# A fused transformer block on one core: the down stage of its FFNs with a fourth split slot, another order of products, and the sum T3 made by an adding DMA

## Chip, cores and metric

The kernel runs on one core of a Trainium2 chip. The metric is the device time of one execution in microseconds. Lower is better.

## What is computed

One block of depth 1 over a sequence of 256 tokens with 2048 channels, all in float32: an FFN, a mixer (sparse attention beside a gated delta rule), and a second FFN, each added to the scaled residual and normalised. The change touches only the two FFNs, and of them only the last product:

```python
D_MODEL = 2048; SEQ = 256; D_FF = 5632

def swiglu(x, w_gate, w_up, w_down):
    return (jax.nn.silu(x @ w_gate) * (x @ w_up)) @ w_down

h = layer_norm(DEEPNORM_ALPHA * h + 0.5 * swiglu(h, ffn1_w_gate[l], ffn1_w_up[l], ffn1_w_down[l]), ...)
```

## The kernel before, in words

**Matmuls of split operands.** Each float32 operand is split into a high and a low part, and a product is three matmuls: high by high, high by low, low by high. The weights come as *raw* tiles of two k-tiles by 512 columns (128 x 1024 elements, 512 KB). SyncE loads them into eight raw slots (L857 in the down stage), ScalarE writes the high part (`split_hi`, L444; `form_hi`, L1054), VectorE the low part as raw minus high (`split_lo`, L451; `form_lo`, L1173), into three split slots (`whi`, `wlo`). TensorE uses them and counts `unit_used`; ScalarE waits on that count before it writes a slot again. SyncE waits for the low half (`lo_done`) of the item that read a raw slot last before it loads that slot again. The queues are in order.

**The down stage.** h (256 tokens x 5632) by w_down (5632 x 2048) is done in two pairs of column chunks: phases F1DA and F1DB in the first FFN, F2DA and F2DB in the second. The class `Pair` (from L50) writes the order of the work out. Its `items` are the work of ScalarE, VectorE and TensorE in order, its `raws` the loads of SyncE in order. An item is either a *unit* (u, c), one raw tile used for both token tiles: 12 matmuls; or one of the products P1 to P7 of a *quad*, 6 matmuls. A quad takes two row tiles a = 4 + q and b = 8 + q and both column chunks of the pair, a 2 by 2 block of weights against a 2 by 2 block of h (two row groups by two token tiles), and makes the eight block products with seven, by Winograd's form of Strassen's scheme. The first pair has three quads, the second four, so there are 14 quads in the kernel.

**The sums of a quad.** VectorE makes four sums of raw weight tiles in `add` (L1146): P5 from (a, 1) and (a, 0) (L1156), P7 from (b, 1) and (a, 1), written over the raw tile (a, 1) (L1159), P6 from (b, 1) and P5's sum (L1162), P4 from (b, 0) and P6's sum (L1167). P5, P6 and P4's sums have a third each of the tile `sumB`. The sums of h (S1 to S4, from A11, A12, A21, A22) are made once in each FFN, beside the first items of the first pair: `sums` (L1195) on VectorE, with `sum_hi` on ScalarE (L1061) and `sum_lo` on VectorE (L1192).

**Order before.** The first pair has 10 units at its head; then a quad lies as unit, P1, P5, unit, P7, P3, unit, P6, P2, unit, P4, and after the last quad come plain units (the tail). P7 and P6's sums are made just before the low half of the item they follow or that is next.

**Folds.** P1, P5, P6 and P7 gather in four PSUM banks `tp`, the others in the units' banks `acc0`, `acc1`. In the tail of each pair ScalarE copies P1's bank (L1083) and VectorE folds the banks into the residual (`fold`, L1252: L1249, L1258, L1261, L1268).

**Edges.** The last six items of the second pair are plain units whose halves go to six slots of their own (`edge`), so that the next phase can start on the split slots.

**Pool.** Pool (GpSimd) has nothing in the down stages but the loads of the norm's gain and bias (`norm_gains`, L778), which wait for a unit of the second pair, and then the norm's reciprocal roots (L783). Its part is written out at L2651 to L2663.

```python
self.raws += [(a, 0), (a, 1), some[0], (b, 1), some[1], (b, 0), *some[2:]]
forms = [("P1", "P5"), ("P7", "P3"), ("P6", "P2"), ("P4",)]
```

## Time and profile before

| | us |
|---|---|
| median of 3 runs | 1941.09 (1940.5 to 1942.88) |
| the profiled execution: its own time | 1941.81 |
| its span, from the first to the last instruction | 1939.8 |
| TensorE busy | 1909.5 (98%) |
| VectorE busy | 1253.9 (65%) |
| ScalarE busy | 894.1 (46%) |
| Pool busy | 66.9 (3%) |
| HBM traffic over the span | 184 GB/s |

The profile's page and the trace's answers give times in us from the span's start. PE is TensorE, PEld its weight loads, DVE VectorE, ACT ScalarE, POOL GpSimd, SP SyncE; L451 is line 451 of the kernel. The first FFN's down stage lies at 495 to 732 us, the second's at 1688 to 1929 us. In an instruction's row, the first number is its start, the second its duration, and the square brackets tell how long the engine was idle before it and what released it.

### The profile page before, as it was taken

The numbers are of one execution on the slowest core, as the hardware profiler recorded it, in microseconds if no ns is written. First come the engines' busy times: TensorE is split into PE (matmuls) and PEld (weight loads), VectorE is DVE, ScalarE is ACT, GpSimd is POOL, SyncE is SP. The second block draws the span as 40 slices with busy tenths as digits, with TensorE's granted clock in tenths as the row PEclk, the third lists the DMA queues.
The fourth block names the chain that finished last, engine by engine and source line by source line (L and its number), as shares of the span: only waits on it lengthen the run. The fifth ranks groups of instructions, "written<-read, shape, count | busy, mean of one in ns | idle before, by whom it ended". The sixth has DMA issues, their size and how long they took to land.

```text
span 1939.8 us, 27987 instructions
## 1 busy us (share of the span) xinstructions
PE 1909.5 (98%) x10490; PEld 1617.4 (83%) x10490; DVE 1253.9 (65%) x1411; ACT 894.1 (46%) x996; POOL 66.9 (3%) x93
## 2 busy tenths in 40 slices
PE   9999999999999999999999999999999999999997
PEld 8888888888778778999999888888888888877776
DVE  5555554555887887676766958555554555587887
ACT  5444443444454553545644544444444444455452
POOL 0000000000000001300131000000000000000000
PEclk9999999999999999999999999999999999999999
DMA  8666666667565665655442067566666666545654
GB/s 304 193 187 189 189 185 189 178 193 235 157 211 182 214 219 171 212 181 161 127 133 89 23 225 243 171 186 182 186 190 197 192 187 188 189 163 184 206 190 168
DMA packets 185365, 357.37 MB, mean 184 GB/s; under 512 B 11328, under 2 KB 23616, under 8 KB 184272
## 3 DMA queue, kind: packets, MB, share of 16 engines
q1 hardware_dynamic: 183600, 347.43, 57.4%
q0 software_dynamic: 1696, 8.99, 1.4%
q8 instruction: 47, 0.77, 0.2%
q14 instruction: 22, 0.18, 0.0%
HBM read 354.28 MB, written 2.10 MB: 184 GB/s over the span
## 4 chain that ended last, share of the span: by engine, by line
PE 91%; DVE 5%; issue 1%; DMA 1%; ACT 1%; POOL 0%; POOLq 0%; SPq 0%; DVEq 0%; ACTq 0%
PE acc L463 23%; PE acc L465 23%; PE acc L464 23%; PE acc L486 3%; PE acc L488 3%; PE acc L490 3%; PE tp L985 1%; PE tp L987 1%; PE tp L986 1%; DVE wlo L451 1%; PE tp L917 1%; PE acc L985 1%; PE acc L987 1%; PE acc L986 1%; ACT whi L444 1%
## 5 line engine op out<-in xcount | busy, mean ns | idle before, releaser
L451 DVE TENSOR_TENSOR wlo<-raw,whi 128x1024 fp32r<-128x1024 f32 (+2 forms) x579 | 692.5, 1202 | 602.8 <-ACT whi L444 600.7
L444 ACT ACTIVATE whi<-raw 128x1024 fp32r<-128x1024 f32 (+2 forms) x579 | 596.6, 1037 | 815.3 <-PE acc L465 726.9
L463 PE MATMUL acc<-whi,xT 128*128 128x512 f32 (+2 forms) x1644 | 631.0, 384 | 0.8 <-ACT zab L1612 0.4
L465 PE MATMUL acc<-whi,xT 128*128 128x512 f32 (+2 forms) x1644 | 625.7, 381 | 0.0
L464 PE MATMUL acc<-wlo,xT 128*128 128x512 f32 (+2 forms) x1644 | 625.2, 380 | 0.0
L463 PEld LDWEIGHTS acc<-whi,xT 128*128 128x128 f32 x1644 | 308.7, 188 | 64.7 <-issue 1.8
L465 PEld LDWEIGHTS acc<-whi,xT 128*128 128x128 f32 x1644 | 308.7, 188 | 59.5
L464 PEld LDWEIGHTS acc<-wlo,xT 128*128 128x128 f32 x1644 | 308.9, 188 | 55.8
L463 PE MATMUL acc<-whi,hT 128*128 128x512 f32 x432 | 170.8, 395 | 6.7 <-DVE wlo L451 6.7
L464 PE MATMUL acc<-wlo,hT 128*128 128x512 f32 x432 | 168.4, 390 | 0.0
L465 PE MATMUL acc<-whi,hT 128*128 128x512 f32 x432 | 168.4, 390 | 0.0
L486 PE MATMUL acc<-xT,whi 128*128 128x256 f32 x384 | 108.7, 283 | 0.0
L488 PE MATMUL acc<-xT,whi 128*128 128x256 f32 x384 | 108.7, 283 | 0.0
L490 PE MATMUL acc<-xT,wlo 128*128 128x256 f32 x384 | 108.7, 283 | 0.0
L463 PEld LDWEIGHTS acc<-whi,hT 128*128 128x128 f32 x432 | 81.1, 188 | 32.8 <-DVE wlo L451 16.4
L465 PEld LDWEIGHTS acc<-whi,hT 128*128 128x128 f32 x432 | 81.1, 188 | 17.4
L464 PEld LDWEIGHTS acc<-wlo,hT 128*128 128x128 f32 x432 | 81.2, 188 | 15.4
L1054 ACT ACTIVATE whi<-raw 128x1024 fp32r<-128x1024 f32 x56 | 59.4, 1061 | 39.3 <-PE acc L465 25.1
L1173 DVE TENSOR_TENSOR wlo<-raw,whi 128x1024 fp32r<-128x1024 f32 x56 | 67.4, 1221 | 11.6 <-ACT whi L1054 10.2
L490 PEld LDWEIGHTS acc<-xT,wlo 128*128 128x128 f32 x384 | 73.7, 192 | 0.0
L488 PEld LDWEIGHTS acc<-xT,whi 128*128 128x128 f32 x384 | 73.7, 192 | 0.0
L486 PEld LDWEIGHTS acc<-xT,whi 128*128 128x128 f32 x384 | 73.7, 192 | 0.0
(345 smaller groups left out, 1854.6 us busy)
## 6 DMA issues: line engine op xcount, KB each, us to landing
raw<-in_ffn_w_down_dram SPq DMA_DIRECT2D x176, 512.0 KB, 4.7
raw<-in_ffn_w_up_dram SPq DMA_DIRECT2D x175, 512.0 KB, 3.7
raw<-in_ffn_w_gate_dram SPq DMA_DIRECT2D x174, 512.0 KB, 3.8
raw<-in_w_in_dram SPq DMA_DIRECT2D x48, 512.0 KB, 3.9
raw<-in_w_out_dram SPq DMA_DIRECT2D x32, 512.0 KB, 6.4
raw<-in_w_in_dram SPq DMA_DIRECT2D x32, 260.0 KB, 2.8
raw<-in_w_in_dram SPq DMA_DIRECT2D x16, 456.0 KB, 5.2
raw<-in_w_q_idx_dram SPq DMA_DIRECT2D x8, 512.0 KB, 3.8
```

The costliest lines, as they stand in the source:

```text
L444: act.activation(hi[:, s, :, 0:w], raw[:, r, :, 0:w], ACT.Copy).then_inc(hi_done, 1)
L451: dve.tensor_tensor(lo[:, s, :, 0:w], raw[:, r, :, 0:w], hi[:, s, :, 0:w].bitcast(F32), ALU.subtract).then_inc(lo_done, 1)
L463: pe.matmul(o, hi, w_hi[:, s, k, 0:width], start=first and k == 0, stop=False)
L464: pe.matmul(o, hi, w_lo[:, s, k, 0:width], start=False, stop=False)
L465: ins = pe.matmul(o, lo, w_hi[:, s, k, 0:width], start=False, stop=last and k == UNIT_KT - 1)
L486: pe.matmul(o, whi[:, s, k, cols], hi, start=first and k == 0 and c == 0, stop=False, skip_group_check=True)
L488: pe.matmul(o, whi[:, s, k, cols], lo, start=False, stop=False, skip_group_check=True)
L490: ins = pe.matmul(o, wlo[:, s, k, cols], hi, start=False, stop=end, skip_group_check=True)
L985: pe.matmul(o, x_hi, w_hi[:, s, k], start=i == touches[0] and k == 0, stop=False)
L986: pe.matmul(o, x_hi, w_lo[:, s, k], start=False, stop=False)
L1054: act.activation(w_hi[:, s], form_raw(p, i), ACT.Copy).then_inc(hi_done, 1)
L1173: dve.tensor_tensor(w_lo[:, s], form_raw(p, i), w_hi[:, s].bitcast(F32), ALU.subtract)\
```

## The change

In each quad the products come in another order: unit, P1, P3, P5, unit, P7, P6, unit, P2, P4, unit. The order of the loads follows. The first pair's head has 13 units instead of 10, and the second pair's last quad four units around it instead of three.

From item 16 of the first pair on (the first quad's P5) there is a fourth split slot, in the room of two of the three parts of `sumB`; it serves both pairs. The remaining part, `form_sum`, holds P5's sum and later P4's. P6's sum is written over the raw tile (a, 0), the *corner*. VectorE waits for both halves of the item that read these places before. The raw tiles (a, 0) and (b, 0) are therefore free only with the item ahead of P4, and (b, 1) with the one ahead of P6.

The signs of the sums are turned so that every weight sum of a quad adds. T3, P7's operand, was (b, 1) - (a, 1) by VectorE and is now (a, 1) + (b, 1): Pool issues a DMA that reads (b, 1) from HBM and adds it onto the raw tile (a, 1), once P5's sum has read it. ScalarE waits for its landing before P7's high half. VectorE's instruction is gone. The signs of two sums of h and of the folds into the second chunk change with it.

The sums of h are spread over items 2 to 14 instead of 2 to 9. VectorE makes a weight sum two items ahead of its product. The folds are eight instructions of 512 columns in place of six and one of 1024.

```diff
-            self.raws += [(a, 0), (a, 1), some[0], (b, 1), some[1], (b, 0), *some[2:]]
-            forms = [("P1", "P5"), ("P7", "P3"), ("P6", "P2"), ("P4",)]
+            self.raws += [some[0], (a, 0), (b, 1), (a, 1), *some[1:3], (b, 0), *some[3:]]
+            forms = [("P1", "P3", "P5"), ("P7", "P6"), ("P2", "P4"), ()]
...
     def released_by(self, r):
-        return max(i for i, (what, _, _) in enumerate(self.items)
-                   if what not in ("P4", "P5", "P6") and self.raw_of(i) == r)
+        last = max(i for i, (what, _, _) in enumerate(self.items)
+                   if what not in ("P4", "P5") and self.raw_of(i) == r)
+        for q, (a, b) in enumerate(self.quads):
+            if self.raws[r] in ((a, 0), (b, 0)):
+                return max(last, self.item("P4", q) - 1)
+            if self.raws[r] == (b, 1):
+                return max(last, self.item("P6", q) - 1)
+        return last
...
+def split_slots(pairs, one_more_from, kept_apart):
+    free, places = list(range(SPLIT_SLOTS)), [{}, {}]
+    user = {}
+    for pair, plan in enumerate(pairs):
+        for i in range(len(plan.items) - (kept_apart if pair else 0)):
+            if (pair, i) == (0, one_more_from):
+                free.insert(0, SPLIT_SLOTS)
+            s = free.pop(0)
+            free.append(s)
+            places[pair][i] = s, user.get(s)
+            user[s] = pair, i
+    return places, user
...
-    PAIRS = [Pair(QUADS[:3], sorted(ENDS + [7, 11]), sorted(ENDS + [7, 11]), 10, (4, 4, 4)),
-             Pair(QUADS, ENDS, ENDS, 2, (4, 4, 4, 3))]
+    PAIRS = [Pair(QUADS[:3], sorted(ENDS + [7, 11]), sorted(ENDS + [7, 11]), 13, (4, 4, 4)),
+             Pair(QUADS, ENDS, ENDS, 2, (4, 4, 4, 4))]
+    FOURTH_FROM = 16
...
+        form_sum = mz("form_sum", 88, [P, UNIT_KT, BANK])
+        fourth_hi = mz("fourth_hi", 92, [P, 1, UNIT_KT, BANK], F32R)
+        fourth_lo = mz("fourth_lo", 96, [P, 1, UNIT_KT, BANK], F32R)
...
+        def down_pool(pool, f, w_down):
+            down_v = w_down.rearrange("(k p) n -> p k n", p=P)
+            for pair, p in enumerate(DOWN[f]):
+                plan = PAIRS[pair]
+                for q, (a, b) in enumerate(plan.quads):
+                    right = raw_ready(pool, p, a, 1)
+                    pool.wait_ge(sem("formed"), made(f, p, "P5", q))
+                    if right_added(f, p, q) > 16:
+                        pool.wait_ge(sem("right_added"), right_added(f, p, q) - 16)
+                    col = (2 * pair + 1) * BANK
+                    pool.dma_start(right, down_v[:, 2 * b:2 * b + 2, col:col + BANK], accum_op=ALU.add)\
+                        .then_inc(sem("right_added"), 16)
...
-                if name in MADE:
+                if name == "P7":
+                    act.wait_ge(sem("right_added"), right_added(f, p, q))
+                elif name in MADE:
                     act.wait_ge(sem("formed"), made(f, p, name, q))
...
                 if name == "P5":
-                    dve.tensor_tensor(sumB[:, 0], upper, left, ALU.subtract).then_inc(sem("formed"), 1)
-                if name == "P7":
-                    block, right = raw_ready(dve, p, b, 1), raw_ready(dve, p, a, 1)
-                    dve.tensor_tensor(right, block, right, ALU.subtract).then_inc(sem("formed"), 1)
+                    dve.tensor_tensor(form_sum[:], upper, corner, ALU.add).then_inc(sem("formed"), 1)
                 if name == "P6":
+                    block = raw_ready(dve, p, b, 1)
+                    dve.wait_ge(lo_done, st.index(p, 0, plan.item("P1", q) + 1))
+                    dve.wait_ge(hi_done, st.index(p, 0, plan.item("P1", q) + 1))
                     dve.wait_ge(sem("formed"), made(f, p, "P5", q))
+                    dve.tensor_tensor(corner, block, form_sum[:], ALU.add).then_inc(sem("formed"), 1)
                 if name == "P4":
                     left = raw_ready(dve, p, b, 0)
+                    dve.wait_ge(lo_done, st.index(p, 0, plan.item("P5", q) + 1))
                     dve.wait_ge(sem("formed"), made(f, p, "P6", q))
-                    dve.tensor_tensor(sumB[:, 2], left, sumB[:, 1], ALU.subtract).then_inc(sem("formed"), 1)
+                    dve.tensor_tensor(form_sum[:], left, corner, ALU.add).then_inc(sem("formed"), 1)
...
-                    if what == "P7":
-                        add(p, "P6", q)
-                    if after[0] == "P6":
-                        add(p, "P4", after[1])
...
+                    soon, of, _ = plan.items[min(i + 2, len(plan.items) - 1)]
+                    if soon in MADE:
+                        add(p, soon, of)
...
+            down_pool(pool, 0, ffn1_w_down[0])
             pool.wait_ge(unit_used, gains_free(0))
             norm_gains(pool, ln1_g, ln1_b)
             norm_pool(pool, 0)
             mixer_pool(pool)
+            down_pool(pool, 1, ffn2_w_down[0])
```

## Rows read from the trace of the kernel before

**Rows 1.** The page, parts 1 and 2: busy time; granted clock in 40 slices.
```profile
PE 1909.5 (98%) x10490; PEld 1617.4 (83%) x10490; DVE 1253.9 (65%) x1411; ACT 894.1 (46%) x996; POOL 66.9 (3%) x93
...
PEclk9999999999999999999999999999999999999999
```

**Rows 2.** Stretches: us, busy of PE, PEld, DVE, ACT, POOL, clock, DMA share, GB/s.
```profile
495.00:610.00 115.00, 112.18 (x494) 91.02 (x493) 97.53 (x89) 59.11 (x57) 0.00 (x0) 1.00 0.53 171
610.00:725.00 115.00, 112.18 (x487) 90.11 (x486) 94.63 (x89) 60.32 (x58) 1.28 (x2) 1.00 0.64 218
554.00:562.00 8.00, 6.89 (x30) 5.37 (x30) 5.21 (x5) 3.90 (x4) 0.00 (x0) 1.00 0.89 269
```

**Rows 3.** TensorE's waits, whole span: us in total, times, longest.
```profile
PE acc L463 <- DVE wlo L451: 6.7, 6, 1.7
PE acc L985 <- DVE wlo L1173: 2.4, 2, 1.2
...
PE acc L463 <- DVE edge L451: 1.6, 2, 0.8
...
PE tp L985 <- DVE wlo L1173: 1.4, 2, 1.1
```

**Rows 4.** Timeline of TensorE: the first matmul behind three of the waits.
```profile
524.90 0.50 PE L463 MATMUL acc<-whi,hT 128*128 128x512 f32 x1 [1.71 <-DVE wlo L451]
...
558.04 0.50 PE L463 MATMUL acc<-whi,hT 128*128 128x512 f32 x1 [1.11 <-DVE wlo L451]
...
673.82 0.47 PE L985 MATMUL acc<-whi,sumA 128*128 128x512 f32 x1 [1.20 <-DVE wlo L1173]
```

**Rows 5.** Timeline of VectorE ahead of the wait at 524.90 us.
```profile
508.28 1.22 DVE L927 TENSOR_TENSOR hT<-tp,hT 128x1024 fp32r<-128x1024 f32 x1
509.42 1.22 DVE L1182 TENSOR_TENSOR sumB<-hT 128x1024 f32<-128x1024 f32 x1
...
523.62 1.22 DVE L451 TENSOR_TENSOR wlo<-raw,whi 128x1024 fp32r<-128x1024 f32 x1
```

**Rows 6.** Timeline of ScalarE and VectorE: halves of units, then of products.
```profile
489.66 1.06 ACT L444 ACTIVATE whi<-raw 128x1024 fp32r<-128x1024 f32 x1 [1.66 <-PE acc L465]
...
490.76 1.23 DVE L451 TENSOR_TENSOR wlo<-raw,whi 128x1024 fp32r<-128x1024 f32 x1 [1.49 <-ACT whi L444]
...
492.38 1.06 ACT L444 ACTIVATE whi<-raw 128x1024 fp32r<-128x1024 f32 x1 [1.66 <-PE acc L465]
...
550.12 1.06 ACT L1054 ACTIVATE whi<-raw 128x1024 fp32r<-128x1024 f32 x1 [0.30 <-PE tp L987]
551.48 1.06 ACT L1054 ACTIVATE whi<-raw 128x1024 fp32r<-128x1024 f32 x1 [0.30 <-PE tp L987]
555.66 1.06 ACT L444 ACTIVATE whi<-raw 128x1024 fp32r<-128x1024 f32 x1 [3.13 <-PE tp L987]
```

**Rows 7.** Groups by line: count, then busy us, mean ns, idle before.
```profile
L1159 DVE TENSOR_TENSOR raw<-raw 128x1024 f32<-128x1024 f32 x14 | 17.0, 1216 | 0.0
...
L1249 DVE SCALAR_TENSOR_TENSOR resid<-sumB,resid 128x512 f32<-128x512 f32 x16 | 10.6, 686 | 0.1
```

**Rows 8.** DMA issues of Pool's queue: count, KB each, median us to landing.
```profile
ln_g<-in_ln_g_dram POOLq DMA_DIRECT2D x3, 1024.0 KB, 8.0
...
wuk<-in_w_uk_dram POOLq DMA_DIRECT2D x1, 1024.0 KB, 5.5
...
cq_g<-in_q_norm_g_dram POOLq DMA_DIRECT2D x1, 256.0 KB, 3.9
```

**Rows 9.** Timeline of Pool: its first load in a down stage.
```profile
706.91 0.74 POOL L778 DMA_DIRECT2D ln_g<-in_ln_g_dram  x1 [705.47 <-PE acc L465]
```

**Rows 10.** The down loads' line, L857, of all down stages.
```profile
DMA to landing us min/median/max: 3.4/4.7/10.3
```

**Rows 11.** Timeline of SyncE's queue, 553 to 555 us.
```profile
553.37 2.02 SPq L857 DMA_DIRECT2D raw<-in_ffn_w_down_dram  x4
```

**Rows 12.** The chain of waits from 608 to 620 us: start, us, what.
```profile
610.56 6.52 DMA raw<-in_ffn_w_down_dram
```

More of the change, by code:

```diff
@@ L71, in __init__ @@
                 self.items += [(form, q, 0) for form in forms[k]]
-        self.tail = len(self.items)
+        self.tail = 1 + max(i for i, item in enumerate(self.items) if item[0] == "P4")
         plain(len(units))
@@ L403, in split_place @@
                 return edge_hi, edge_lo, slot, st.index(p, 0, edge_free(slot))
+            if plan_of(p) is not None:
+                f, pair = (0, 1)[p in DOWN[1]], (0, 1)[p in (F1DB, F2DB)]
+                s, before = SPLITS[pair][u] if u < n else (u - n, LAST_USER[u - n])
+                if before is not None:
+                    free = st.index(DOWN[f][before[0]], 0, before[1] + 1)
+                elif s < SPLIT_SLOTS:
+                    last = [v for v in range(2 * KU) if ring_place(v, 2 * KU, SPLIT_SLOTS) == s][-1]
+                    free = st.index(GU[f], GATE_CHUNKS - 1, last + 1)
+                else:
+                    free = None
+                return (whi, wlo, s, free) if s < SPLIT_SLOTS else (fourth_hi, fourth_lo, 0, free)
             if p in EXITS and isinstance(it, int) and it == st.phases[p].iters - 1:
@@ L882, in made, with right_added @@
             pair = DOWN[f].index(p)
-            return F_STEPS * f + len(SUM_STEPS) + sum(PAIR_STEPS[:pair]) + 4 * q + MADE[name]
+            return F_STEPS * f + len(SUM_STEPS) + sum(PAIR_STEPS[:pair]) + ADDS * q + MADE[name]
         def folded(f, pair, n):
-            return F_STEPS * f + len(SUM_STEPS) + sum(PAIR_STEPS[:pair]) + 4 * len(PAIRS[pair].quads) + n
+            return F_STEPS * f + len(SUM_STEPS) + sum(PAIR_STEPS[:pair]) + ADDS * len(PAIRS[pair].quads) + n
+        def right_added(f, p, q):
+            pair = DOWN[f].index(p)
+            quads = [len(plan.quads) for plan in PAIRS]
+            return 16 * (sum(quads) * f + sum(quads[:pair]) + q + 1)
+        def down_pool(pool, f, w_down):
[10 more added lines that the diff above has]
+                        .then_inc(sem("right_added"), 16)
         def p_free(f, pair):
@@ L1052, in form_hi @@
                     act.wait_ge(raw_loaded[v % RAW_SLOTS], st.loaded(p, 0, v))
-                act.wait_ge(unit_used, free)
+                if free is None:
+                    act.wait_ge(sem("formed"), summed(f, "S4 low"))
+                else:
+                    act.wait_ge(unit_used, free)
                 act.activation(w_hi[:, s], form_raw(p, i), ACT.Copy).then_inc(hi_done, 1)
@@ L1146, in add @@
             def add(p, name, q):
-                first = p == DOWN[f][0] and q == 0
-                a, b = plan_of(p).quads[q]
+                pair, plan = DOWN[f].index(p), plan_of(p)
+                a, b = plan.quads[q]
+                corner = raw_ready(dve, p, a, 0)
                 if name == "P5":
-                    upper, left = raw_ready(dve, p, a, 1), raw_ready(dve, p, a, 0)
-                    if first:
-                        dve.wait_ge(sem("formed"), summed(f, "S4 low"))
-                    elif q == 0:
-                        dve.wait_ge(sem("formed"), folded(f, 0, FOLDS))
-                    dve.tensor_tensor(sumB[:, 0], upper, left, ALU.subtract).then_inc(sem("formed"), 1)
@@ L1157, in add @@
-                if name == "P7":
-                    block, right = raw_ready(dve, p, b, 1), raw_ready(dve, p, a, 1)
-                    dve.tensor_tensor(right, block, right, ALU.subtract).then_inc(sem("formed"), 1)
+                    upper = raw_ready(dve, p, a, 1)
+                    if q > 0:
+                        dve.wait_ge(lo_done, st.index(p, 0, plan.item("P4", q - 1) + 1))
+                        dve.wait_ge(hi_done, st.index(p, 0, plan.item("P4", q - 1) + 1))
+                    else:
+                        dve.wait_ge(sem("formed"), folded(f, 0, FOLDS) if pair else summed(f, "S4 low"))
@@ L1288, in down_pair @@
                 for i in range(LEAD if pair == 0 else 0, len(plan.items)):
-                    what, q, _ = plan.items[i]
-                    after = plan.items[i + 1] if i + 1 < len(plan.items) else ("", 0, 0)
-                    if after[0] == "P1":
-                        add(p, "P5", after[1])
-                    if what == "P5":
-                        add(p, "P7", q)
-                    if what == "P7":
-                        add(p, "P6", q)
-                    if after[0] == "P6":
-                        add(p, "P4", after[1])
-                    if what == "unit":
+                    if plan.items[i][0] == "unit":
                         split_lo(dve, p, 0, i)
```

79 lines of the change are left out of this document (44 added, 35 removed).

## Prediction

> **What bounds the kernel now.** I read the page first, then the stages, then the waits inside the down stages. TensorE is busy 98% of the span and the granted clock is full, 2.4 GHz [rows 1]. So only TensorE's idle time can be won, and only work that makes TensorE late can cost. The two halves of the first down stage show 112.2 us of matmuls in 115 us each, with VectorE at 95 to 98 us of 115 [rows 2]. TensorE's waits name the rest: over both down stages 6.7 + 2.4 + 1.6 + 1.4 = 12.1 us, all released by VectorE's low half of a split [rows 3]. They fall on a unit behind the sums, on items behind P4 and on an edge unit; the larger ones of the first stage are the rows at 524.90, 558.04 and 673.82 us, and the second stage repeats them [rows 4]. These 12.1 us are the whole prize (the first matmul behind a wait also takes 0.50 instead of 0.39 us [rows 4], so up to 2 us more).
>
> The mechanism of one item: ScalarE's high half starts when a slot comes free, takes 1.06 us, VectorE's low half starts 1.10 us after it and takes 1.23 us, and back to back VectorE needs 1.14 us per instruction [rows 5, 6]. A unit (12 matmuls) holds TensorE 2.72 us and a product (6) 1.36 us, the spacing of ScalarE's starts in the two cases [rows 6]. The work on TensorE is the same before and after: the same units and the same seven products a quad.
>
> **The change, part by part.**
>
> *The sums of the second operand and the head of 13 units.* Before the longest stall, VectorE works without a break from 508.28 on, and the low half of the unit at 523.62 comes 1.7 us late [rows 5, 4]. The sums are the same number of instructions, but now lie over items 2 to 14, with the P5 sum behind item 14. A unit with two instructions costs VectorE 2.28 us against 2.72 us of TensorE, and the few items with three catch up before item 14. I take this stall (1.7 us, once per down stage) as gone; the bound is that it stays.
>
> *One VectorE instruction fewer a quad.* The T3 subtraction (L1159) is 1.22 us, 14 times [rows 7], 16 us of VectorE at the back-to-back pace. What it covers is only the stalls above; VectorE has idle time otherwise. The folds become eight instructions of 0.68 us instead of six and one of full size, 1.22 us [rows 7]: 0.14 us more, four times, beside TensorE's work; nothing, and 0.1 us at the kernel's end if that cover were gone.
>
> *The fourth slot.* Before the stall at 558 us ScalarE waited 3.1 us for TensorE to free a slot [rows 6], and VectorE then for ScalarE; the one at 674 us is of this kind [rows 4]. A slot more lets the high half go one item earlier, 1.36 us or more. I take these as gone too. It exists only from item 16 on, when the last low half of S4 is written. The new waits of the P5, P6 and P4 sums are for halves that stand earlier in VectorE's own queue, as the sums share one buffer and the corner's block: they hold nothing up, and their price is the raw slots kept longer, below.
>
> *The adding DMA.* Nothing like it is in the trace, so it is bounded. It is issued by Pool behind the P5 sum, because that sum reads the block which the DMA overwrites; ScalarE's half of P7 waits for its landing, and behind that wait ScalarE holds P6, a unit, P2 and P4, and VectorE all their low halves. Pool's queue has nothing else in the down stages; the gains' loads come at 706.91 us [rows 9], behind the last adding DMA, so they don't collide. Landings of Pool's DMAs: 3.9 us for 256 KB, 5.5 us for 1 MB, 8.0 us for 1 MB beside the down stage's own loads [rows 8]. The adding DMA writes 512 KB but must read 1 MB, the weights and the block. Lower end: it costs as a plain 512 KB, between 3.9 and 5.5, so 4.4 us; upper end: 8.0 us, as the 1 MB beside loads. I take 7.0 us, nearer to the rows with contention, since the 16 DMA engines are 53 to 64% busy there [rows 2]; with 0.2 us for the two semaphores D = 7.2 us from P5's sum to the landing. Issuing costs Pool 0.7 us of it [rows 9] and no other engine.
>
> The Trainium skill (DMA: Bandwidth & Descriptors, Anatomy of one DMA) gives 2.0 us plus bytes at 436 GB/s for a DMA of this queue, 4.4 us for the 1 MB; the trace has 5.5 to 8.0 us for 1 MB, and the trace decides. The skill (Collectives: The Full Stack, The bandwidth ceiling) says that an adding transfer is half as fast since it needs two source reads, not because of the addition; no row here shows it.
>
> *What covers it.* The first quad still has three slots, and its P5 sum stands behind P1's low half and S4's. ScalarE starts P1's high half 0.2 us after TensorE begins the unit two before P1, 5.4 us ahead of P1. Then 1.3 us to the low half (with a little queueing), 1.14 to S4's, 1.25 to the P5 sum, 1.23 for it: it ends 5.1 us after that point, 0.3 us before P1 starts. P1, P3, P5 and a unit last 3 x 1.36 + 2.72 = 6.8 us, and P7's two halves need 2.4 us ahead of P7. Cover: 0.3 + 6.8 - 2.4 = 4.7 us. D = 7.2 exceeds it by 2.5 us.
>
> In later quads there is a loop. The new order releases six loads at once, when P2's low half of the quad before is done: the blocks at its corner and left are kept for the sums until then, and the queue is in order. The third load of the six is the block (a, 1), which the P5 sum needs. A load alone lands in 3.4 us at least [rows 10]; in a burst of four issued from 553.37 us on [rows 11] the 8 us that follow move 269 GB/s [rows 2], which is 1.95 us per 512 KB; at 400 GB/s it would be 1.3; I take 1.6. The third lands 0.2 + 3.4 + 3.2 = 6.8 us after the release. Then: P5 sum 1.25; adding DMA D; P7's halves 2.4; VectorE's four instructions up to P2's low half (P6, unit, the P4 sum, P2) 4 x 1.13 = 4.5. The loop is 6.8 + 1.25 + 2.4 + 4.5 + D = 15.0 + D. TensorE's quad is 4 x 2.72 + 7 x 1.36 = 20.4 us. So D may be 5.4 us; with 7.2 the stall is 1.8 us a quad.
>
> **Sum.** Loops: 2 in the first pair, 3 in the second, 5 x 1.8 = 9 us; the first quad 2.5 us; the second pair's first quad has units ahead of it and the P5 sum early, 0. That makes 11.5 us a down stage, 23 us for both. Taken away: 12.1 us. Net +10.9 us. The profiled execution took 1941.8 us (span 1939.8 and 2.0 around it), 0.7 us over the median of 1941.1; so 1952.7 by the profile, 1952 as a median.
>
> **The rivals.**
>
> *Covered (the other side).* If D is at most 4.7 us and the burst lands as fast as single loads, no stall of either kind is left: 1941.1 - 12.1 - 2 = 1927. For it: 3.9 us for 256 KB, 5.5 us for 1 MB [rows 8], and nothing in the trace forbids the adding unit to run at the rate of a load. With D from 4.7 to 5.4 only the first quad stalls, at most 0.7 us twice. Against it: six loads are in the queue just then, and a Pool DMA beside loads took 8.0 us [rows 8]. The point from which it decides: D plus the third load's landing under about 12 us. The skill's 4.4 us of the DMA page, taken as it is, would give this case; the rows so far bear it out badly. Chance 0.34.
>
> *Balance.* D about 6.2 us: 5 x 0.8 + 1.5 = 5.5 us a down stage, 11 for both against 12.1: 1940. The same result comes if the change doesn't do what it says, the old stalls staying because ScalarE gets no slot in time, and the DMA just covered. Chance 0.15.
>
> *The loads become the bound.* The burst of six behaves as the loads at 610 us did: issued one behind the other, the one that ScalarE waited for took 6.5 us [rows 12], and the worst down load of the kernel 10.3 us [rows 10]. If the third of six lands at 8.5 instead of 6.8 and slows the adding DMA to 7.8: loop 24.5, stall 4.1 a quad, 5 x 4.1 + 3.1 = 24 us a stage, 47 against 12: 1976. ScalarE's waits would then name the plain loads too. Chance 0.13.
>
> *Forecast* (D 6.5 to 8.2): 1943 to 1964 by the same sum, 12 us of kernel time per us of D (10 from the loops, 2 from the first quads). Chance 0.38.
>
> **Numbers.** The likeliest case gives 1952 us. The range takes in the covered case (1927, and 1925 with the slowed matmuls) and goes up to 1968, past D = 8.2; most of the loads' case lies above. A measurement of this kernel tells 0.2%, 3.9 us, from no change. Faster: 0.34 and a little of the balance, 0.35. Same: 0.14. Slower: 0.38 + 0.13, 0.51. Cases of both signs hold most of the chance; the forecast's own range is 1943 to 1964.
>
> **What would show it.** The rows of Pool should have 14 issues into the raw tile with a time to landing: 7 us for my forecast, under 5 for the covered case. ScalarE's waits should have a new group on these DMAs, of 1 to 3 us each, and TensorE idle ahead of the P7 products (the line of the products, into the transposes' tile) 12 times. The waits on VectorE's low halves at the old places (the unit behind the sums, the unit behind P4, the edge) should be gone; if one stays, its part above is wrong. SyncE should issue six loads within 2.5 us once a quad, and the landings of the down loads should rise above their median of 4.7 us [rows 10]. If TensorE shows no idle time ahead of P7 while the DMA takes 7 us, my loop is wrong, not D. If the stall is there and the DMA lands in 5 us, it is the loads.

## The result, and the profile after

The changed kernel takes **1964.8 us** (median of 4 runs, 1964.45 to 1966.21). The kernel before, on the same chip, takes 1941.9 us (4 runs, 1940.5 to 1942.88). The ratio is 1.012, with a 95% interval from 1.0102 to 1.0138: slower by 23 us. The forecast was 1952 us, in a range from 1925 to 1968 us. The sign was right. The size was not: +23 us against a forecast of +10.9 us. The profiled execution took 1966.2 us, with a span of 1964.5 us. Two versions below had one slow execution each among their ten (5191 us in experiment 4, 2342 us in experiment 11); comparisons leave these out.

The page of the changed kernel, the lines that answer to [rows 1, 7, 8] (parts 1, 2, 5 and 6):

```profile
PE 1918.1 (98%) x10490; PEld 1629.1 (83%) x10490; DVE 1239.9 (63%) x1401; ACT 889.6 (45%) x996; POOL 83.8 (4%) x107
...
L1121 ACT ACTIVATE whi<-raw 128x1024 fp32r<-128x1024 f32 x54 | 56.2, 1054 | 78.8 <-DMA raw<-in_ffn_w_down_dram 67.9
...
L949 POOL DMA_DIRECT2D raw<-in_ffn_w_down_dram x14 | 17.0, 1216 | 1371.3 <-DVE form_sum L1226 844.0
...
raw<-in_ffn_w_down_dram SPq DMA_DIRECT2D x176, 512.0 KB, 6.8
...
raw<-in_ffn_w_down_dram POOLq DMA_DIRECT2D x14, 512.0 KB, 7.6
```

VectorE has 14 us less work and TensorE the same 10,490 matmuls, yet these are 8.6 us *longer* in sum than in [rows 1]. ScalarE stands for 67.9 us before high halves that come from raw tiles. The plain down loads land in 6.8 us in the median, against 4.7 us in [rows 10]. The 14 adding DMAs land in 7.6 us, and an issue costs Pool 1.2 us instead of the 0.74 us of [rows 9].

TensorE's waits, whole span, the lines that answer to [rows 3]: us in total, times, longest.

```profile
PE tp L1047 <- DVE wlo L1243: 26.3, 10, 4.5
...
PE tp L1047 <- DVE fourth_lo L1243: 2.9, 2, 1.7
...
PE tp L616 <- DVE resid L781: 0.8, 1, 0.8
```

L1047 into `tp`, released by a product's low half (L1243), is P7. None of the places of [rows 3] is left; in their stead P7 is late 12 times, by 26.3 + 2.9 = 29.2 us in all. The timeline of one such place, the second quad of the first stage, for ScalarE, VectorE and Pool:

```profile
552.07 1.06 ACT L1121 ACTIVATE whi<-raw 128x1024 fp32r<-128x1024 f32 x1 [2.11 <-DMA raw<-in_ffn_w_down_dram]
...
554.80 1.23 DVE L1226 TENSOR_TENSOR form_sum<-raw 128x1024 f32<-128x1024 f32 x1 [0.42 <-DMA raw<-in_ffn_w_down_dram]
...
556.59 1.22 POOL L949 DMA_DIRECT2D raw<-in_ffn_w_down_dram  x1 [20.57 <-DVE form_sum L1226]
...
564.13 2.00 ACT L1121 ACTIVATE whi<-raw 128x1024 fp32r<-128x1024 f32 x2 [6.02 <-DMA raw<-in_ffn_w_down_dram]
```

P1's block has landed at 552.07 us. The P5 sum runs from 554.80 to 556.03 us. The square brackets say that the sum was released by a load's landing, the block (a, 1), and not by VectorE's own queue. Pool issues the adding DMA 0.56 us later, and ScalarE can start P7's high half at 564.13 us, 8.1 us behind the sum. TensorE in the same place:

```profile
566.59 0.77 PE L1047 MATMUL tp<-whi,sumA 128*128 128x512 f32 x1 [2.84 <-DVE wlo L1243]
567.16 0.63 PE L1048 MATMUL tp<-wlo,sumA 128*128 128x512 f32 x1
567.58 0.63 PE L1049 MATMUL tp<-whi,sumA 128*128 128x512 f32 x1
```

This is what the forecast had no term for. Behind a wait of 2.84 us the matmuls take 0.63 us each and start 0.43 us apart, where they otherwise take 0.39 us and start 0.23 us apart. The windows of TensorE show why: us, busy, granted clock, DMA share, GB/s.

```profile
495.00:610.00 115.00, 108.90 (x476) 0.99 0.59 183
610.00:725.00 115.00, 108.11 (x461) 0.97 0.66 216
...
566.60:570.10 3.50, 3.50 (x9) 0.53 0.02 5
570.20:590.00 19.80, 18.63 (x82) 1.00 0.75 238
705.40:710.00 4.60, 4.60 (x13) 0.63 0.00 0
```

The granted clock falls to its lower level, 1.2 GHz, for a few us, and is back at 2.4 GHz after that. This happens behind six of the twelve waits: those of 2.84, 1.86 and 3.64 us in the first stage and of 4.45, 4.28 and 3.54 us in the second. In the profile of before it happens in no down stage; the first two windows had a clock of 1.00 in [rows 2]. A spell (a stretch of matmuls at the lower level) holds about eight slow matmuls in the first stage and ten to thirteen in the second, 0.20 us more each. That is 1.6 us a spell and 2.0 to 2.6 us, some 12 us altogether.

Not all of these 12 us are a cost, as the starts of the first three P7 show:

```profile
543.10 0.47 PE L1047 MATMUL tp<-whi,sumA 128*128 128x512 f32 x1 [2.02 <-DVE wlo L1243]
...
566.59 0.77 PE L1047 MATMUL tp<-whi,sumA 128*128 128x512 f32 x1 [2.84 <-DVE wlo L1243]
...
590.08 0.47 PE L1047 MATMUL tp<-fourth_hi,sumA 128*128 128x512 f32 x1 [1.25 <-DVE fourth_lo L1243]
```

From the first to the second lie 23.49 us without a spell, from the second to the third 23.49 us with one. The spell made the next wait shorter (1.25 us instead of 2.84), not the quad longer. What sets P7's start runs through the loads, the P5 sum, the adding DMA and the halves, and not through TensorE: in all ten later quads the first load of the quad's burst is issued 6.9 us after the high half of the P7 before started, with a spell in between or without. Only a spell behind the last P7 of a pair costs in full. Two of the six are such (705.38 and 1912.81 us), some 4 us.

**The balance of TensorE's time.** This sum says where TensorE's time went, not what caused it. Waits 29.2 - 12.1 = +17.1 us, and +12 us of clock. Against that go the small delays at the old places, which the waits of [rows 3] don't hold. Between the starts of TensorE's matmuls, the first stage of before shows 9.0 us of gaps where its waits sum to 5.6 us: behind each wait the first matmul is longer, and where a unit follows a product the unit's first two come 0.1 us late each. The new waits bring 0.24 us each of this kind, 1.4 us a stage. That makes -2 us a stage, and the wait at the next norm's transposes (L616) is 1.1 us shorter. 17 + 12 - 4 - 1 = 24 us, against 23 measured.

By cause it reads otherwise. In the ten quads that have a quad ahead of them in their pair, P7 starts 22.4 to 25.3 us after the P7 before, 24.0 us in the mean, where TensorE's work is 20.4 us: 36 us in all. The two first quads add 4 us and the spells behind the last P7 some 4 us. Against these 44 us stand some 18 us of idle time won (experiment 1).

### The profile page after: what moved, and what is told of

Read it like the earlier page. It is cut to its first block, busy times and chain, and to the rows that moved or that the text cites. A ratio compares the mean times of both kernels' runs of the same rounds, so it can differ in the third digit from the quotient of the medians.

```text
span 1964.5 us, 28033 instructions
## 1 busy us (share of the span) xinstructions
PE 1918.1 (98%) x10490; PEld 1629.1 (83%) x10490; DVE 1239.9 (63%) x1401; ACT 889.6 (45%) x996; POOL 83.8 (4%) x107
## 4 chain that ended last, share of the span: by engine, by line
PE 79%; DMA 10%; DVE 7%; issue 2%; ACT 1%; POOL 0%; POOLq 0%; DVEq 0%; SPq 0%; ACTq 0%
PE acc L505 21%; PE acc L507 21%; PE acc L506 21%; DMA raw<-in_ffn_w_down_dram 9%; PE acc L528 3%; PE acc L530 3%; PE acc L532 3%; DVE wlo L1243 2%; PE tp L979 1%; DVE wlo L493 1%; DVE form_sum L1226 1%; DVE form_sum L1237 1%; DVE fourth_lo L1243 1%; ACT whi L1121 1%; PE tp L2566 1%
## 5 line engine op out<-in xcount | busy, mean ns | idle before, releaser
L493 DVE TENSOR_TENSOR wlo<-raw,whi 128x1024 fp32r<-128x1024 f32 (+2 forms) x559 | 668.1, 1201 | 587.8 <-ACT whi L486 586.5
L486 ACT ACTIVATE whi<-raw 128x1024 fp32r<-128x1024 f32 (+2 forms) x559 | 575.2, 1036 | 750.5 <-PE acc L507 677.7
L505 PE MATMUL acc<-whi,hT 128*128 128x512 f32 x352 | 137.7, 391 | 0.0
L506 PE MATMUL acc<-wlo,hT 128*128 128x512 f32 x352 | 137.0, 389 | 0.0
L507 PE MATMUL acc<-whi,hT 128*128 128x512 f32 x352 | 137.0, 389 | 0.0
L1243 DVE TENSOR_TENSOR wlo<-raw,whi 128x1024 fp32r<-128x1024 f32 x54 | 65.2, 1221 | 50.5 <-ACT whi L1121 50.4
L1121 ACT ACTIVATE whi<-raw 128x1024 fp32r<-128x1024 f32 x54 | 56.2, 1054 | 78.8 <-DMA raw<-in_ffn_w_down_dram 67.9
L505 PEld LDWEIGHTS acc<-whi,hT 128*128 128x128 f32 x352 | 66.7, 189 | 14.0
L506 PEld LDWEIGHTS acc<-wlo,hT 128*128 128x128 f32 x352 | 66.5, 189 | 13.9
L507 PEld LDWEIGHTS acc<-whi,hT 128*128 128x128 f32 x352 | 66.1, 188 | 13.9
L949 POOL DMA_DIRECT2D raw<-in_ffn_w_down_dram x14 | 17.0, 1216 | 1371.3 <-DVE form_sum L1226 844.0
L530 PEld LDWEIGHTS acc<-xT,whi 128*128 128x128 f32 x384 | 72.8, 189 | 0.0
```

Source lines behind the costliest of these rows:

```text
L486: act.activation(hi[:, s, :, 0:w], raw[:, r, :, 0:w], ACT.Copy).then_inc(hi_done, 1)
L493: dve.tensor_tensor(lo[:, s, :, 0:w], raw[:, r, :, 0:w], hi[:, s, :, 0:w].bitcast(F32), ALU.subtract).then_inc(lo_done, 1)
L505: pe.matmul(o, hi, w_hi[:, s, k, 0:width], start=first and k == 0, stop=False)
L506: pe.matmul(o, hi, w_lo[:, s, k, 0:width], start=False, stop=False)
L507: ins = pe.matmul(o, lo, w_hi[:, s, k, 0:width], start=False, stop=last and k == UNIT_KT - 1)
L530: pe.matmul(o, whi[:, s, k, cols], lo, start=False, stop=False, skip_group_check=True)
```

## The experiments

The theory: the adding DMA is slower than its cover, and all that the rest of the change wins is real. The main rival: the six loads released at once are the bound, with or without this DMA.

**1. T3 on VectorE, all else kept.**

```diff
-                if name == "P7":
-                    act.wait_ge(sem("right_added"), right_added(f, p, q))
-                elif name in MADE:
+                if name in MADE:
...
+                if name == "P7":
+                    block, right = raw_ready(dve, p, b, 1), raw_ready(dve, p, a, 1)
+                    dve.tensor_tensor(right, block, right, ALU.add).then_inc(sem("formed"), 1)
...
-            down_pool(pool, 0, ffn1_w_down[0])
```

> The changed kernel with T3 made by VectorE again (now as an addition into the raw tile (a, 1)), and no adding DMA; order, fourth slot, spread sums and in-place sums stay. Theory A (the adding DMA lands too late for P7, and nothing else of the change costs): the 29 us of TensorE's waits at P7 go, and with them the 0.43 us matmul spacing that follows the longer ones; 1927 to 1932 us. Theory B (the late release of raw tiles makes bursts of loads, and these are what is late): 1950 us or more, with ScalarE waiting for plain loads. Theory C (the new order was itself a gain that the DMA hides): faster than before by the 12 us of VectorE's stalls, so A's number; if the order brought nothing, 1941.

Measured: **1924.5 us** (4 runs), ratio to before 0.9904 [0.9887, 0.992], clock 0.998. In its down stages TensorE's waits are nearly gone:

```profile
PE acc L505 <- DVE wlo L493: 1.1, 3, 0.4
...
PE tp L616 <- DVE resid L781: 0.6, 1, 0.6
```

The plain loads land in 6.5 us in the median here too, and nothing waits for them long enough to matter. So the burst alone is harmless, and the adding DMA in this order turns 18 us won into 23 us lost. The time lies 2.5 us below the range of theory A. This version beats both kernels.

**2. The same DMA without the addition.**

```diff
-                    pool.dma_start(right, down_v[...], accum_op=ALU.add)\
+                    pool.dma_start(right, down_v[...])\
```

> The changed kernel, but Pool's DMA loads (b, 1) over the raw tile (a, 1) without adding: same issue, same waits, one read instead of two. (T3 is left out: P7 multiplies (b, 1) alone.) If the second read makes the DMA late: landing 4.5 to 6 us instead of 7.6, and 1935 to 1945 us. If it is the queue it shares with the plain loads and the fixed part: landing stays above 7 us and the time above 1955.

Measured: 1952.6 us (one run), clock 0.994. Landing, from the line's own view:

```profile
DMA to landing us min/median/max: 4.2/6.2/7.3
```

The changed kernel's line has 5.7/7.6/9.0. The addition adds 1.4 us to the landing and 0.5 us to Pool's issue (0.72 against 1.20 us). P7's waits fall from 29.2 to 19.1 us. Both the landing and the time lie between the numbers of the two theories: a plain 512 KB of this queue still takes 6.2 us here, so the addition is the smaller part of D.

**3. P7 two operations later.**

```diff
-            forms = [("P1", "P3", "P5"), ("P7", "P6"), ("P2", "P4"), ()]
+            forms = [("P1", "P3", "P5"), ("P6",), ("P7", "P2", "P4"), ()]
```

> The changed kernel with P7 two places later (P1, P3, P5, unit, P6, unit, P7, P2, P4, unit), so that 1.36 + 2.72 = 4.1 us more of TensorE's work lie between P5's sum and P7. Theory A: the landing (5.7 to 9.0 us) is then covered by 8.8 to 10 us, the waits at P7 go almost entirely; 1928 to 1937 us. Theory B: waits remain, at P7 or at the plain loads' items, above 1950 us.

Measured: 1934.3 us (4 runs), ratio 0.9958 [0.9942, 0.9975], clock 0.998. The landing is nearly as in the changed kernel (5.9/7.4/9.5), and of P7's waits one of 0.4 us is left. What costs 40 us over experiment 1 in one place costs 10 us in another: most of it is a matter of cover. What the last 10 us are was not settled.

**4. Three slots (experiment 1 without the fourth).**

```diff
-    FOURTH_FROM = 16
+    FOURTH_FROM = 10 ** 9
```

> As e1 (T3 by VectorE), but without the fourth split slot. If the fourth slot is what removes the stalls behind P4: 3 to 6 us over e1, with VectorE waiting for ScalarE and ScalarE for TensorE ahead of TensorE's waits. If the order and the earlier sums do it alone: within 1 us of e1.

Measured: 1943.1 us, ratio 1.0001 [0.9991, 1.0011]. Stalls of the kind of [rows 3], units held up by VectorE's low halves, are back, smaller and more of them:

```profile
PE acc L505 <- DVE wlo L493: 7.2, 14, 0.7
```

The first wait of this run's down stage is this one; the 1.71 us of 524.90 us [rows 4] is gone:

```profile
539.16 0.47 PE L505 MATMUL acc<-whi,hT 128*128 128x512 f32 x1 [0.66 <-DVE wlo L493]
```

So the spread sums and the head of 13 units do take away the stall behind the sums, but the new order brings as much in small ones, and without the fourth slot nothing is won: 18.6 us over experiment 1, where 3 to 6 had been expected. The slot in the old order was not run.

**5. The right block loaded first.**

```diff
-            self.raws += [some[0], (a, 0), (b, 1), (a, 1), *some[1:3], (b, 0), *some[3:]]
+            self.raws += [some[0], (a, 0), (a, 1), (b, 1), *some[1:3], (b, 0), *some[3:]]
```

> The changed kernel with one pair of loads swapped: the raw tile (a, 1) is loaded ahead of (b, 1). Theory A1 (in the later quads the P5 sum, and so the adding DMA, is held up by the third of six loads released at once): P5's sum and the adding DMA start earlier by one load of the burst, 1.3 to 1.9 us, in 10 of 14 quads; TensorE's waits at P7 fall from 29 to 12 to 17 us, fewer stretches at half clock, 1940 to 1950 us. Rival (only the DMA's own time counts, P5's sum waits for VectorE's queue): within 3 us of the changed kernel, 1962 to 1966.

Measured: 1962.4 us (4 runs), ratio 1.0096 [1.008, 1.0113]. P7's waits sum to 27.7 us. The rival's number came out, but the sum does move. In the second quad:

```profile
553.51 1.22 DVE L1243 TENSOR_TENSOR wlo<-raw,whi 128x1024 fp32r<-128x1024 f32 x1 [2.28 <-ACT whi L1121]
554.65 1.22 DVE L1226 TENSOR_TENSOR form_sum<-raw 128x1024 f32<-128x1024 f32 x1
```

The P5 sum no longer waits for a load; it follows P1's low half at once, which waits for the *first* load of the burst through P1's high half. In the changed kernel it had waited for (a, 1), the third load, in all ten later quads, for 0.3 to 1.5 us beyond that low half. So the third load was the gate, with the first close behind it. Counted from the issue of the burst's first load, the sum now starts at 6.6 us instead of 7.6 (medians of the ten), but the adding DMA takes 9.0 us to land instead of 7.8, and is there at 17.3 us instead of 17.2. The microsecond won ahead of the DMA is lost inside it.

**6. The kernel before, with the adding DMA alone.**

```diff
+            down_pool(pool, 0, ffn1_w_down[0])
...
-                    if what == "P5":
-                        add(p, "P7", q)
```

> The kernel before with the adding DMA alone: Pool adds (b, 1) onto (a, 1) behind the P5 sum, VectorE's T3 instruction goes, order, slots and sums stay. (T3 is a sum there where a difference is wanted.) In this order the P5 sum is made a unit earlier, ahead of the unit before P1: from its end to P7's high half lie 7.0 us of TensorE's work, against 4.7 to 6.2 in the changed kernel. If the landing is 7.5 us again, a wait of 0.5 to 1.5 us at each P7 comes on top of before's waits: 1945 to 1960 us. If the adding DMA costs the same wherever it stands (2 us a quad): 1970.

Measured: 1942.1 us (one run; before on this chip 1942.7 us). Neither expected number came (1945 to 1960, or 1970): the same 14 DMAs cost nothing in the old order. They land sooner there:

```profile
DMA to landing us min/median/max: 5.6/5.9/10.1
```

5.9 us against 7.6 us for the same instruction and bytes. So D isn't a property of the transfer alone. Two things differ in the old order: the P5 sum stands a unit ahead of P1, and the loads come spread out, where the changed kernel issues eight or nine back to back from 547.5 us on. Experiments 9, 11 and 12 take these apart.

**7. P7 late with no DMA at fault.** The next two start from experiment 1, where TensorE hardly waits, and make it wait for ScalarE.

```diff
+                if name == "P7":
+                    for k in range(4):
+                        again[0] += 1
+                        act.activation(w_hi[:, s], form_raw(p, i), ACT.Copy).then_inc(sem("again"), 1)
+                        act.wait_ge(sem("again"), again[0])
                 act.activation(w_hi[:, s], form_raw(p, i), ACT.Copy).then_inc(hi_done, 1)
```

> The kernel with T3 made on VectorE and no adding DMA, with one thing more: ScalarE makes the high half of P7 four extra times (about 1.06 us each and a little between them) ahead of the time that counts, so P7 comes about 4.5 to 5 us late in all 14 quads with nothing changed in the transfers. Theory W (the granted clock falls because TensorE itself stood still for long enough): P7 waits of 1 to 4 us, as in the changed kernel, and behind the longer ones matmuls 0.43 us apart for some us, with a granted clock of 0.985 to 0.993 over the span; time 1945 to 1965 us. Theory T (the fall comes with the heavier traffic of the adding DMA): the same waits, but every matmul behind them at 0.227 us and the clock at 0.998; time 1940 to 1955 us.

Measured: 1971.6 us, clock 0.992, 14 waits of 31.4 us in all:

```profile
PE tp L1047 <- DVE wlo L1253: 23.2, 10, 2.7
PE tp L1047 <- DVE fourth_lo L1253: 8.2, 4, 2.6
```

The granted clock falls behind seven of the waits, one of 1.90 us and six of 2.57 to 2.65 us. The time is 7 us above theory W's range, which had been drawn too low for 31.4 us of waits and seven spells on top of 1924.5 us. The clock is inside its own range: the fall needs no adding DMA.

**8. The same with six extra makings** (`range(6)`).

> As the run before with six extra makings of P7's high half, so each wait about 2.3 us longer. Theory W: nearly every P7 wait (4 to 6 us) is followed by a spell at the half level, 12 to 14 spells; clock 0.975 to 0.988, and the time over the four-times version grows by more than 14 x 2.3 = 32 us, to 1980 to 2010 us. Theory T: clock 0.998 and growth of 32 us at most, to 1970 to 1985 us.

Measured: 2010.5 us, clock 0.981, 14 waits of 55.2 us in all, and 14 spells at the lower level. The growth over run 7 is 39 us. The added waiting is 23.8 us of it, 1.7 us a wait; the rest goes with the clock. Here a spell costs in full: in ten of the 14 quads ScalarE's extra work is released by TensorE freeing the slot, so the slow matmuls delay the next P7 too. A row of ScalarE's timeline shows the release by TensorE, two of TensorE's the first spell, and a window another (us, busy of PE, clock, DMA share, GB/s):

```profile
589.09 6.52 ACT L1126 ACTIVATE fourth_hi<-raw 128x1024 fp32r<-128x1024 f32 x6 [0.30 <-PE tp L1049]
```

```profile
546.44 0.76 PE L1047 MATMUL tp<-whi,sumA 128*128 128x512 f32 x1 [4.76 <-DVE wlo L1253]
547.00 0.63 PE L1048 MATMUL tp<-wlo,sumA 128*128 128x512 f32 x1
```

```profile
598.10:604.00 5.90, 5.89 (x14) 0.50 0.08 7
```

Theory T, that the fall comes with the adding DMA's traffic, is out: there is no such DMA here, and the DMA share is 0.08 in that window.

**9. The P5 sum one operation earlier** (and the loads as in 5).

```diff
+                    soon, of, _ = plan.items[min(i + 3, last_item)]
+                    if soon == "P5" and of > 0:
+                        add(p, soon, of)
```

> The changed kernel with the P5 sum put one operation earlier in VectorE's order (ahead of P1's low half) in every quad that isn't the first of its pair, and the right block's load moved ahead of the lower-right block's, so that the Pool queue can issue its adding DMA some 1.5 to 2 us sooner. Theory C (cover alone decides: the order of before hid this DMA because its P5 sum stood a unit earlier): 9 or 10 of the 12 P7 waits get 1.5 to 2 us shorter, and the half-level spells behind them mostly go: 29 us of waits fall to 12 to 18, time 1938 to 1950 us. Rival L (the blocks of the burst land when they land, 552.1 us at the earliest in the second quad, and an earlier place on VectorE gains under 0.5 us a quad): 1957 to 1965 us.

Measured: 1958.8 us (4 runs), ratio 1.0085 [1.0068, 1.0102]. The rival's number, but not for its reason. Pool's issue did come 2.0 us sooner, and the landing took 9.1 us instead of 7.6:

```profile
554.59 1.22 POOL L949 DMA_DIRECT2D raw<-in_ffn_w_down_dram  x1 [19.09 <-DVE form_sum L1226]
```

```profile
563.70 2.00 ACT L1121 ACTIVATE whi<-raw 128x1024 fp32r<-128x1024 f32 x2 [5.87 <-DMA raw<-in_ffn_w_down_dram]
```

Issued at 554.59 us it is there at 563.70 us; issued at 556.59 us, at 564.13 us. Two us of earlier issue bring 0.4. The waits sum to 28.5 us, hardly less than 29.2, and there are four spells instead of six (clock 0.995 against 0.990). Yet the 6 us that this version is faster are not mainly the clock's: the ten distances from P7 to P7 sum to 234.3 us instead of 240.0, which is 5.7 us. The loop has become shorter, and with fewer slow matmuls in it TensorE shows more of it as waiting.

**10. The same, with P7 later as in 3.**

> The run before with P7 also moved behind a unit, two operations later in the order of products (P6 alone in the second group, P7, P2, P4 in the third). P7 two later alone took 1934.3 us. Theory C: what small waits are left there (3.9 us over its down stages) mostly go: 1929 to 1933 us, still over the 1924.5 us of the kernel without this DMA, since its extra traffic delays the raw loads. Rival L: no difference from 1934.3 us beyond 2 us, or slower, as the earlier sum holds up P1's low half behind the right block's landing.

Measured: 1930.5 us (4 runs), ratio 0.9938 [0.9922, 0.9955]. Theory C's number came (1929 to 1933). But the interval overlaps that of experiment 3, so the 4 us between them aren't settled. The landing is 8.9 us in the median, and covered but for one wait of 0.4 us.

**11. Fewer loads beside it.** Run 9 asked whether the adding DMA waits for the loads that are under way. Here SyncE holds back the last loads of the burst:

```diff
+                    held = [q for q, (_, b) in enumerate(plan.quads) if q > 0 and (u, c) == (b, 0)]
+                    if held:
+                        sp.wait_ge(sem("right_added"), right_added(f, p, held[0]))
                     sp.dma_start(raw[:, s], down_v[...]).then_inc(raw_loaded[s], 16)
```

> The changed kernel with one wait more on SyncE's queue: from each pair's second quad on, the load of the block that P2 needs, and all loads behind it, are issued only when the quad's adding DMA has landed. Two or three of the burst's loads so move behind it. Theory Q (the adding DMA lands when the loads ahead of it have been served, so an earlier issue only makes it longer: 7.6 us from the old place, 9.1 us when issued 1.5 to 2 us sooner): its landing falls to 5.5 to 6.5 us, the 12 waits for P7 from 29 to 12 to 20 us, the half-level spells mostly go: 1942 to 1954 us. Rival F (the landing is a fixed cost of the two reads and of Pool's queue): landing 7.3 to 8 us, waits as they were, and the held loads come late besides: 1964 to 1975 us.

Measured: **1943.5 us**, ratio 1.0006 [0.9996, 1.0016]. Its landings, and TensorE's waits:

```profile
DMA to landing us min/median/max: 5.7/5.8/6.9
```

```profile
PE tp L1050 <- DVE wlo L1246: 13.7, 9, 2.6
PE tp L1050 <- DVE fourth_lo L1246: 2.4, 2, 1.5
```

Landing 7.6 to 5.8 us, waits 29.2 to 16.1 us, one spell at the lower clock instead of six: 21 us won by three lines that only *delay* loads. All three are in theory Q's ranges. The windows of the second quad, first of the changed kernel, then of this one (us; busy of PE, PEld, DVE, ACT, POOL; clock; DMA share; GB/s):

```profile
550.00:556.00 6.00, 6.00 (x28) 4.99 (x27) 3.63 (x4) 2.12 (x2) 0.00 (x0) 1.00 1.02 370
556.00:562.00 6.00, 6.00 (x28) 4.96 (x27) 4.66 (x5) 2.05 (x2) 1.22 (x1) 1.00 1.08 342
```

```profile
556.00:562.00 6.00, 6.00 (x28) 4.99 (x27) 4.67 (x5) 2.10 (x2) 1.22 (x1) 1.00 0.66 117
562.00:568.00 6.00, 4.74 (x21) 3.60 (x21) 4.28 (x4) 3.80 (x4) 0.00 (x0) 1.00 0.69 219
```

In the changed kernel the DMA engines are full while the adding DMA is in flight; in this one they are at two thirds, and the held loads use the time behind it. In both Pool issues it at the same time, 556.59 and 556.60 us.

**12. Fewer loads and the earlier sum.**

> As the run before, with the P5 sum one operation earlier and the right block loaded ahead of the lower-right one. Theory Q: with fewer loads beside it the adding DMA can use the earlier issue, landing 6 to 7.5 us instead of 9.1, waits 8 to 18 us, time 1934 to 1948 us. Rival F: landing over 8.5 us and 1955 to 1970 us.

Measured: 1933.0 us (4 runs), ratio 0.9948 [0.9931, 0.9964], landing 6.2 us in the median, P7's waits 7.6 us, no spell at the lower clock. The waits and the time are better than theory Q's ranges, by 0.4 and 1 us. With fewer loads beside it the earlier issue does count, which it hardly did in run 9:

```profile
554.76 1.22 POOL L952 DMA_DIRECT2D raw<-in_ffn_w_down_dram  x1 [18.94 <-DVE form_sum L1229]
```

```profile
560.90 2.01 ACT L1124 ACTIVATE whi<-raw 128x1024 fp32r<-128x1024 f32 x2 [3.00 <-DMA raw<-in_ffn_w_down_dram]
```

| kernel | us | landing of Pool's DMA, median | P7 waits | clock |
|---|---|---|---|---|
| changed | 1964.8 | 7.6 | 29.2 | 0.990 |
| 9, sum early | 1958.8 | 9.1 | 28.5 | 0.995 |
| 2, no addition | 1952.6 | 6.2 | 19.1 | 0.994 |
| 11, loads held | 1943.5 | 5.8 | 16.1 | 0.997 |
| 3, P7 later | 1934.3 | 7.4 | 0.4 | 0.998 |
| 12, held and early | 1933.0 | 6.2 | 7.6 | 0.998 |
| 1, T3 on VectorE | 1924.5 | - | 0 | 0.998 |

The ten later quads by themselves, from the traces' rows: us after the issue of the burst's first load (medians), and the distance from one P7 to the next (mean).

| kernel | P5 sum starts | DMA takes | DMA has landed | P7 to P7 |
|---|---|---|---|---|
| changed | 7.6 | 7.8 | 17.2 | 24.0 |
| 5, right block first | 6.6 | 9.0 | 17.3 | 23.9 |
| 9, sum early | 5.8 | 9.1 | 16.8 | 23.4 |
| 11, loads held | 7.4 | 5.8 | 15.2 | 21.9 |
| 12, held and early | 5.7 | 6.4 | 14.2 | 20.9 |

With all loads of the burst in flight the DMA has landed at about 17 us, whenever it was issued; only with the last loads held back does it come sooner.

## Why the prediction was right or wrong

**What bounds the kernel.** Right: only TensorE's idle time moved the result, in every run. Incomplete: behind some of the waits TensorE's clock fell as well.

**The prize of 12.1 us (up to 14).** Too small. Experiment 1 wins 18.4 us. The waits of [rows 3] count from a matmul's end; from start to start, all gaps of the down stages of before are some 17 us. The small delays between a product and a unit, about 0.2 us each, are in no row of waits.

**The sums and the head of 13 units take away the first stall, the fourth slot the others.** Right as to the places: the stall at 524.90 us is gone even without the slot (experiment 4). Wrong as to what it is worth: without the slot the new order's own small stalls take all of it back, and the time stays at that of before.

**The T3 instruction, the folds, the waits of the sums: nothing.** Right. Experiment 1 puts the 14 instructions back on VectorE and has no stall from them; it has the folds and the sums' new waits as well.

**D = 7.2 us.** This is the term that failed most. Over all 14 DMAs the landing is 7.6 us in the median (7.0 taken), and the hops on both sides are nearer 0.6 than 0.2 us. In the ten later quads, where the term counts ten times, D is 7.8 to 9.6 us, 8.5 us in the mean: 1.3 us over the forecast. In the two first quads it is 6.6 and 6.3 us. The reason for taking the upper rows was right, contention with the loads, but I had it as one fixed number for quads with a burst beside them and quads without. The landing's median goes from 5.8 to 9.1 us with what else is in flight and when it is issued.

The Trainium skill (DMA: Bandwidth & Descriptors, Anatomy of one DMA) gives an estimate of 3.2 us for the plain 512 KB. The trace of experiment 2 has 6.2 us in the median, with 4.2 us as its least. The Trainium skill (Collectives: The Full Stack, The bandwidth ceiling) puts a ReduceScatter at half the rate of an AllGather because its add needs two source reads. As a factor on the landing of one DMA that isn't borne out: the addition is 1.4 us of 7.6. As the time of one more read of 512 KB it fits: by the 436 GB/s of the Trainium skill's page on DMA that is 1.2 us, an estimate.

**Pool's issue at 0.7 us.** 1.2 us for the adding form, 0.72 us without the addition. It lies within the landing's time.

**The cover of the first quad, 4.7 us, stall 2.5 us.** The cover was right: 6.6 us of D less 2.0 us of stall in the first stage, 6.3 less 1.7 in the second, are 4.6 us in both. The stalls are smaller than forecast because D is.

**The loop of later quads, stall 1.8 us.** The mechanism was right: the place, the count (12 waits, none in the second pair's first quad), and the chain. The step that failed is the size of the stall: P7 comes 24.0 us after the P7 before instead of 22.2, so a quad loses 3.6 us and not 1.8, and ten of them 36 us and not 18. Two terms of the loop's sum failed:

| term | forecast | measured in the ten later quads, mean |
|---|---|---|
| burst's first load to the start of the P5 sum (third load) | 6.8 | 7.6 |
| P5 sum | 1.25 | 1.2 |
| D | 7.2 | 8.5 |
| P7's halves, then VectorE to P2's low half | 6.9 | 6.9 |
| loop | 22.2 | 24.2 |

(The distances' mean is 24.0 and not 24.2, since the first loop of a stage's second pair starts from a P7 that is not late.) The third load is the gate as forecast, 0.8 us later, with the first load through P1's low half close behind it. D is the larger miss. Experiments 5, 9, 11 and 12 show why: the burst fills the DMA engines until about 562 us in the quad shown, and the adding DMA lands when they come free.

**No term for the clock.** A miss, but a smaller one than its 12 us suggest. Experiments 7 and 8 show the lower level behind waits with no such DMA in the kernel. In the changed kernel the spells between two P7 of a pair are taken up by the next wait; an estimate of what is left is the two spells behind the last P7, some 4 us.

**The rivals.** "Covered" did not come true, but its mechanism is the one that experiments 3 and 12 realise: put P7 later, or D down with an earlier sum, and the kernel is faster than before. "Loads become the bound" is out in the form given; experiment 1 has the same burst and no stall. Its effect through the adding DMA is real. Its 47 us of stalls are in fact nearer to the measured 44 us than the forecast's 23 us; what keeps the time below its 1976 us is the prize, 18 us instead of 12. So two misses partly cancel: with the forecast's prize the measured stalls would have given some 1971 us, an estimate, beyond the range. That 1965 us lies within it is in part luck.

**The signs to look for.** 14 issues near 7 us, 12 waits ahead of P7, the old places empty, the median of the plain landings risen to 6.8 us: all as written. The sixth load of a burst is issued 2.6 to 3.9 us after the first, not within 2.5 us. ScalarE's waits on these DMAs were expected at 1 to 3 us each and are up to 7.5 us, since ScalarE runs ahead of TensorE.

What stays open: why the clock falls behind some waits of 2.6 us and not behind others of 2.7 us, what makes experiment 3 10 us slower than experiment 1, whether experiments 3 and 10 differ, and what the fourth slot would win in the old order.

## What to carry to other kernels

Moving an operation from an engine with idle time to a DMA only pays if its landing is covered, and the cover must be reckoned with the loads that will be in flight at that moment. Where a late transfer shares the engines with a burst that isn't urgent, issuing it sooner can win little (0.4 us of 2.0 in experiment 9), while holding back the burst's last loads won 21 us (experiment 11). Price a stall by the loop that sets it. If the loop doesn't pass through TensorE, slow matmuls at the lower clock only shorten the next wait, and the waits' sum hides what was won or lost; compare the distance from one such place to the next. If it does pass through TensorE, as in experiment 8, a long stall costs itself and up to 2.6 us again.

## What the hardware did that I had not expected

- The granted clock fell to half behind waits of TensorE of 1.9 to 4.8 us and stayed there for some eight to thirteen matmuls. In run 8 all 14 waits (3.7 to 4.8 us) had such a spell, in run 7 seven of 14 (1.5 to 2.7 us), and in run 9 a wait of 3.7 us had none.
- A DMA of Pool's queue, issued 2.0 us sooner into full DMA engines, landed 0.4 us sooner (run 9); with the burst's last loads held back, it took 5.8 us from issue to landing in the median instead of 7.6 (run 11).
- The adding form costs Pool 1.20 us to issue against 0.72 us, and 1.4 us more to land.
